# The inverse of the delta rule's triangular matrices, levelled from the left side instead of the right, on one core

## The chip, the cores and the metric

The kernel runs on one core of one Trainium2 chip. The metric is the device time of one execution of the whole program in microseconds (us). The program computes two transformer blocks one after the other; the change touches one stage of the first block, which runs twice.

## The reference, cut to what matters

The first block's mixer is a gated delta rule in chunks of 64 tokens. For each chunk, head and direction a unit lower triangular 64x64 matrix is made and a system with it is solved.

```python
def gated_delta_chunked(q, k, v, beta, g, s0):
    incl, strict = tri_masks()
    q, k, v, beta, g = map(to_chunks, (q, k, v, beta, g))
    gc = jnp.cumsum(g, axis=-1)
    decay = jnp.exp(jnp.where(incl, gc[..., :, None] - gc[..., None, :], -jnp.inf))
    kk = jnp.einsum("nbhid,nbhjd->nbhij", k, k)
    a_mat = jnp.where(strict, beta[..., :, None] * kk * decay, 0.0) + jnp.eye(CHUNK, dtype=kk.dtype)
    ...
    sol = lax.linalg.triangular_solve(a_mat, rhs, left_side=True, lower=True, unit_diagonal=True)
    ...
    def step(s, xs):
        qd, kd, u_c, w_c, qk_c, al = xs
        v_new = u_c - jnp.einsum("bhck,bhkv->bhcv", w_c, s)
        ...
```

There are 8 heads of width 128, 256 context tokens and 512 latent tokens (12 chunks), and two directions, of which the second reads the tokens backwards.

## The kernel before

**Stages.** The heads are worked in two groups of four (hg 0 and 1). For each group `pe_chunks`, `act_chunks`, ... project, convolve and normalise; then `pe_scan`, `act_scan`, `dve_scan` and `pool_scan` run the delta rule. The change lies in the scans alone. All the engines' queues are written out by hand, each engine in program order; semaphores join them.

**Units.** A scan has 12 units, s = 0 to 11. A unit is one chunk of each direction for four heads: the chunk of one direction lies on partitions 0 to 63, that of the other on 64 to 127, so that a tile of 128x256 holds eight 64x64 matrices. A block of matmuls over them is 8 instructions of 64x64 (4 heads by 2 halves), each shown by the profile as two records of fp32, 16 records a block. Units 0 to 3 are context, 4 to 11 (`lat`) are latent and have two phases more (`qk` and `pt`). Each unit uses one of four sets of tiles: XY (X in columns 0 to 255, Y = X transposed in 256 to 511), BA (A, and beside it its transpose AT), EP (E, PP), EQ and R. In the rows all of these are called `u`; the identity, masks and other constants are `con`, the level masks `lvl`.

**What a unit does.** `ga` and `kk` make A: POOL `ga`, PE k times k and a sum of gates, ACT exp (`ev`), POOL times beta (`eb`), DVE product (`a`). `tr` makes the start of the inverse: POOL X = A times the level 0 mask (`x0`), DVE X += identity (`xy` 0), and beside them PE turns A (block `at`) and ACT copies AT from PSUM to SBUF. Then five levels, each in two phases. `("ax", lv)`: PE multiplies A by X, DVE masks it into E (`ev`). `("xy", lv)`: PE makes both products of E with the inverse (two blocks, 32 records), DVE adds them to X and Y. In `("ax", 1)` PE also turns X (block `y0`), and ACT copies that to Y. After the levels `ks`, `vn` and `out` apply the inverse, and update the states SS (`ss` in the rows: 8 SCALAR_TENSOR_TENSOR on DVE for a unit).

**Order.** `gdn_order` sets one order of phases for all engines. It works in turns: in a turn each live unit does its next phase, oldest first, and the newest unit is last. Two to four units are live. So in the turn in which a new unit has its `tr`, the blocks and DVE steps of the older units stand ahead of it in every queue.

**PSUM.** The 8 banks are a ring: `K.ps.take` waits until the readers of the bank's last but eighth user have let go.

Of the kernel before, what the change touches and what calls it, by code (L numbers as in the profile page):

```python
# [373 lines left out]
class Kernel:  # L374
# [958 lines left out]
    def pe_scan(self, hg):  # L1333
        K, pe, hs = self, self.pe, range(4)
        H = lambda ap, h: ap[:, h * 128:h * 128 + 128]
        Q = lambda ap, h: ap[:, h * 64:h * 64 + 64]
        act, dve, pool, id_ = K.act, K.dve, K.pool, K.con("id")
        rows = [slice(64 * hf, 64 * hf + 64) for hf in range(2)]
        pe.wait_ge(K.ended("chunks", hg), dve.at("nbe"))
        for s, ph in gdn_order():  # L1340
            par, lat, (XY, BA, EP, EQ, R) = K.unit(s)
            z, inc, pair = (hg, s), K.con(f"inc{par}"), K.pair(s)
            X, Y, A, AT, E, PP = XY[:, 0:256], XY[:, 256:512], BA[:, 0:256], BA[:, 256:512], EP[:, 0:256], EP[:, 256:512]
            tok = [slice(c * 64, c * 64 + 64) for _, _, c in pair]
            if ph == "kk":
                b = K.ps.take(pe, "kk", *z)
# [6 lines left out]
            elif ph == "qk":  # L1353
                b = K.ps.take(pe, "gq", *z)
                for h in hs:
                    pe.mm(H(b, h), K.col(K.gg, s, hg, h).broadcast_to([128, 128]), inc)
                pe.mark("gq", *z)
                b = K.ps.take(pe, "qk", *z)
                for h in hs:
                    for d, hf, c in pair:  # L1360
                        pe.mm(Q(b, h)[rows[hf], :], K.QT[:, h, (c - 4) * 64:(c - 3) * 64], K.KT[:, h, tok[d]])
                pe.mark("qk", *z)
            elif ph == "tr":
                if s == 0:
                    K.pe_keep(3, "ramp", hg)
                b = K.ps.take(pe, "at", *z)
                pe.wait_ge(dve.at("a", *z))
                for h in hs:
                    for r in rows:
                        pe.mm(Q(b, h)[r, :], Q(A, h)[r, :], id_[r, r])  # L1370
                pe.mark("at", *z)
            elif ph == "pt":
                b = K.ps.take(pe, "pt", *z)
                pe.wait_ge(dve.at("p", *z))
                for h in hs:
                    for r in rows:
                        pe.mm(Q(b, h)[r, :], Q(PP, h)[r, :], id_[r, r])
                pe.mark("pt", *z)
            elif ph[0] == "ax":
                lv = ph[1]  # L1380
                b = K.ps.take(pe, "ax", *z, lv)
                pe.wait_ge(act.at("at", *z), dve.at("xy", *z, lv - 1))
                for h in hs:
                    for r in rows:
                        pe.mm(Q(b, h)[r, :], Q(AT, h)[r, :], Q(X, h)[r, :])
                pe.mark("ax", *z, lv)
                if lv == 1:
                    b = K.ps.take(pe, "y0", *z)
                    for h in hs:
                        for r in rows:  # L1390
                            pe.mm(Q(b, h)[r, :], Q(X, h)[r, :], id_[r, r])
                    pe.mark("y0", *z)
            elif ph[0] == "xy":
                lv = ph[1]
                b = K.ps.take(pe, "xy", *z, lv)
                pe.wait_ge(dve.at("ev", *z, lv), act.at("y0", *z))
                for h in hs if lv < 5 else ():
                    for r in rows:
                        pe.mm(Q(b, h)[r, :], Q(Y, h)[r, :], Q(E, h)[r, :])
                for h in hs:  # L1400
                    for r in rows:
                        pe.mm(Q(b, 4 + h)[r, :], Q(E, h)[r, :], Q(Y, h)[r, :])
                pe.mark("xy", *z, lv)
            elif ph == "ks":
                b = K.ps.take(pe, "ks", *z)
                pe.wait_ge(dve.at("s", hg, s - 1))
                for h in hs:
                    for d, hf, c in pair:
                        pe.mm(H(b, h)[rows[hf], :], K.KT[:, h, tok[d]], H(K.SS[:, d, :], h))
                pe.mark("ks", *z)  # L1410
            elif ph == "vn":
                b = K.ps.take(pe, "vn", *z)
                pe.wait_ge(act.at("bv", *z) if s == 0 else dve.at("r", *z), dve.at("xy", *z, 5))
                for h in hs:
                    for r in rows:
                        pe.mm(H(b, h)[r, :], Q(Y, h)[r, :], H(R, h)[r, :])
                pe.mark("vn", *z)
                if lat:
                    b = [K.ps.take(pe, "o", *z, d) for d in range(2)]
                    pe.wait_ge(pool.at("q", *z))  # L1420
                    for h in hs:
                        for d, hf, c in pair:
                            pe.mm(Q(b[d], h), H(K.SS[:, d, :], h), EQ[:, h * 128 + hf * 64:h * 128 + hf * 64 + 64], h == 0, False,
                                  skip=True)
                    pe.mark("os", *z)
            elif ph == "out":
                if s < 11:
                    b = [K.ps.take(pe, "s", *z, d) for d in range(2)]
                    pe.wait_ge(dve.at("vd", *z))
                    for h in hs:  # L1430
                        for d, hf, c in pair:
                            pe.mm(H(b[d], h), K.KM[rows[hf], c // 2, h * 128:h * 128 + 128], H(R, h)[rows[hf], :])
                    pe.mark("s", *z)
                if lat:
                    b = [K.ps["o", hg, s, d] for d in range(2)]
                    pe.wait_ge(act.at("vn", *z), act.at("pt", *z))
                    for h in hs:
                        for d, hf, c in pair:
                            pe.mm(Q(b[d], h), H(BA, h)[rows[hf], :], Q(PP, h)[rows[hf], :], False, h == 3, skip=True)
                    pe.mark("o", *z)  # L1440
                pe.mark("unit", *z)
# [7 lines left out]
    def act_scan(self, hg):  # L1449
# [3 lines left out]
        for s, ph in gdn_order():  # L1453
# [8 lines left out]
                act.a(EQ, K.ps[("gq", *z)], ACT.Exp).then_inc(act("eq", *z), 1)  # L1462
                act.also("ps", "gq", *z)
            elif ph == "tr":
                act.wait_ge(pe.at("at", *z))
                act.cp(BA[:, 256:512], K.ps[("at", *z)][:, 0:256]).then_inc(act("at", *z), 1)
                act.also("ps", "at", *z)
            elif ph == "pt":
                act.wait_ge(pe.at("pt", *z))
                act.cp(EP[:, 256:512], K.ps[("pt", *z)][:, 0:256]).then_inc(act("pt", *z), 1)  # L1470
                act.also("ps", "pt", *z)
            elif ph[0] == "ax":
                h = ph[1] - 1
                if h == 0:
                    act.wait_ge(pe.at("y0", *z))
                    act.cp(XY[:, 256:512], K.ps[("y0", *z)][:, 0:256]).then_inc(act("y0", *z), 1)
                    act.also("ps", "y0", *z)
                for d, hf, c in K.pair(s) if h < 4 else ():
                    r = slice(64 * hf, 64 * hf + 64)
                    v, o = K.VM[r, c // 2, h * 128:h * 128 + 128], R[r, h * 128:h * 128 + 128]  # L1480
# [15 lines left out]
    def dve_scan(self, hg):  # L1496
# [5 lines left out]
        for s, ph in gdn_order():  # L1502
# [15 lines left out]
            elif ph[0] == "ax":  # L1518
                lv = ph[1]
                dve.wait_ge(pe.at("ax", *z, lv), dve.at("p" if lat else "a", *z) if lv == 1 else pe.at("xy", *z, lv - 1))  # L1520
                b, m = K.ps[("ax", *z, lv)][:, 0:256], K.lvl[:, lv * 2 + par, :]
                dve.tt(q4(E), q4(b), bc4(m), ALU.mult).then_inc(dve("ev", *z, lv), 1)
                dve.also("ps", "ax", *z, lv)
            elif ph[0] == "xy":
# [1881 lines left out]
```

## Time and profile before

| | us |
|---|---|
| median of 3 runs | 3894.75 (3884.72 to 3899.01) |
| the profiled execution, its span | 3889.4 |
| scan of group 0, about 254 to 461 us of the span | 207 |
| scan of group 1, about 595 to 804 us of the span | 209 |

The profiled execution has no time of its own beside its span. The scans are 416 us of 3889, and in each 12 units are inverted. The rest (projections, attention, feed-forward) has none of the changed lines. The profile of a scan is read by its timeline, since all matmuls are recorded at one line, that of a helper (L208), as are the two-operand steps (L239) and the activations (L227).

### The profile page before, as it was taken

What the parts mean: (1) busy time and instruction counts of PE and PEld (TensorE: products, weight loads), DVE (VectorE), ACT (ScalarE), POOL (GpSimd) and SP (SyncE); (2) the same over time, 40 slices, a digit from 0 to 9 for tenths busy, and PEclk for the clock granted to TensorE, in tenths of its full rate; (3) what the DMA queues carried; (4) which work ended last, traced back from release to release, by engine and by line L of the source; (5) the groups of instructions that cost most, each with busy time, mean ns of one, the idle gap of its engine ahead of it and who ended that gap; (6) DMA issues with size and microseconds to landing.
All of it is one profiled execution on the core that took longest, in us unless ns stands there. A gap on an engine that the chain in (4) does not pass through costs nothing.

```text
span 3889.4 us, 60956 instructions
## 1 busy us (share of the span) xinstructions
PE 3713.0 (95%) x25674; PEld 3011.8 (77%) x25674; DVE 1933.2 (50%) x2996; ACT 1516.2 (39%) x2548; POOL 845.8 (22%) x842
## 2 busy tenths in 40 slices
PE   6999899999999999998999999999999899999999
PEld 4678787987888757786888788876778688878887
DVE  6656555535444565745243543447565533454343
ACT  5533233323323356735233432235575522343222
POOL 1222122121111133442110120203344321002120
PEclk8999999989999999999999999999999999999999
DMA  6310030012222202111224122221111122222222
GB/s 240 121 43 3 19 70 3 3 64 105 97 96 96 71 28 76 61 60 49 94 96 137 63 93 98 98 82 39 66 60 60 35 96 98 103 92 98 95 96 91
DMA packets 81543, 300.88 MB, mean 77 GB/s; under 512 B 8824, under 2 KB 9976, under 8 KB 80504
## 3 DMA queue, kind: packets, MB, share of 16 engines
q1 hardware_dynamic: 80240, 294.90, 21.8%
q10 hardware_dynamic: 1032, 2.10, 0.5%
q8 instruction: 203, 3.33, 0.3%
q14 instruction: 68, 0.56, 0.0%
HBM read 292.76 MB, written 4.19 MB: 76 GB/s over the span
## 4 chain that ended last, share of the span: by engine, by line
PE 74%; DVE 11%; ACT 6%; issue 5%; POOL 3%; DMA 1%; SPq 0%; DVEq 0%; POOLq 0%; ACTq 0%
PE ps L208 73%; DVE wlo L239 1%; DVE he L247 1%; ACT whi L227 1%; DVE ac L247 1%; PE ps L213 1%; ACT ha L227 1%; POOL p L243 1%; DVE hc L2476 1%; ACT L227 1%; ACT wp L228 1%; DVE ss L247 1%; DVE ws L247 1%; DVE ha L239 1%; DVE sml L1944 0%
## 5 line engine op out<-in xcount | busy, mean ns | idle before, releaser
L239 DVE TENSOR_TENSOR wlo<-wraw,whi 128x1024 fp32r<-128x1024 f32 x537 | 689.8, 1289 | 777.4 <-ACT whi L227 776.7
L208 PE MATMUL ps<-hh,whi 128*128 128x512 f32 x1840 | 732.0, 398 | 6.5 <-ACT hh L227 2.1
L208 PE MATMUL ps<-hl,whi 128*128 128x512 f32 x1840 | 722.6, 393 | 0.0
L208 PE MATMUL ps<-hh,wlo 128*128 128x512 f32 x1840 | 722.0, 392 | 0.0
L227 ACT ACTIVATE whi<-wraw 128x1024 fp32r<-128x1024 f32 x537 | 559.6, 1049 | 207.7 <-PE ps L208 171.8
L208 PEld LDWEIGHTS ps<-hh,whi 128*128 128x128 f32 x1840 | 348.9, 190 | 90.9 <-ACT hh L227 7.7
L208 PEld LDWEIGHTS ps<-hh,wlo 128*128 128x128 f32 x1840 | 349.1, 190 | 74.2
L208 PEld LDWEIGHTS ps<-hl,whi 128*128 128x128 f32 x1840 | 349.5, 190 | 70.2
L208 PE MATMUL ps<-u,u 64*64 64x64 f32 (+2 forms) x6016 | 223.7, 226 | 25.5 <-DVE u L239 15.4
L208 PEld LDWEIGHTS ps<-u,u 64*64 64x64 f32 (+1 forms) x6016 | 204.7, 137 | 41.6 <-DVE u L239 19.4
L239 POOL TENSOR_TENSOR sml<-sml,con 128x4 f32<-128x4 f32 (+3 forms) x36 | 66.4, 1847 | 640.3 <-DVE sml L244 579.1
L208 PE MATMUL ps<-gh,wlo 128*128 128x512 f32 x528 | 205.5, 389 | 0.0
L208 PE MATMUL ps<-gl,whi 128*128 128x512 f32 x528 | 205.5, 389 | 0.0
L208 PE MATMUL ps<-gh,whi 128*128 128x512 f32 x528 | 205.5, 389 | 0.0
L227 ACT ACTIVATE u<-ps 128x256 f32<-128x256 f32 (+1 forms) x128 | 57.6, 450 | 251.2 <-PE ps L208 185.3
L208 PE MATMUL ps<-fh,whi 128*128 128x512 f32 x352 | 137.6, 391 | 3.3 <-ACT fh L227 2.3
L208 PE MATMUL ps<-fh,wlo 128*128 128x512 f32 x352 | 137.0, 389 | 0.0
L208 PE MATMUL ps<-fl,whi 128*128 128x512 f32 x352 | 137.0, 389 | 0.0
L239 POOL TENSOR_TENSOR gl<-fv,gh 128x512 fp32r<-128x512 f32 x66 | 85.3, 1293 | 232.1 <-ACT gh L227 232.1
L239 DVE TENSOR_TENSOR x<-x,ps 128x512 f32<-128x512 f32 x64 | 44.0, 688 | 172.7 <-PE ps L208 172.7
L227 ACT ACTIVATE gh<-fv 128x512 fp32r<-128x512 f32 x66 | 41.7, 632 | 213.4 <-DVE fv L239 213.4
L239 POOL TENSOR_TENSOR fs<-fs,rb 128x512 f32<-128x512 f32 x44 | 56.9, 1293 | 301.9 <-ACT fg L227 301.9
(402 smaller groups left out, 7062.6 us busy)
## 6 DMA issues: line engine op xcount, KB each, us to landing
wraw<-weights SPq DMA_DIRECT2D x537, 512.0 KB, 3.2
x<-xT SPq DMA_DIRECT2D x2, 2048.0 KB, 9.5
bias_lines<-ln ACTq DMA_DIRECT2D x1, 2048.0 KB
xmf<-memT SPq DMA_DIRECT2D x2, 1024.0 KB, 4.7
out<-x SPq DMA_DIRECT2D x4, 512.0 KB, 2.6
bias<-bias_lines SPq DMA_DIRECT2D x1, 1536.0 KB, 8.3
con<-consts SPq DMA_DIRECT2D x1, 1379.0 KB, 16.5
ctxt<-ctxT SPq DMA_DIRECT2D x1, 1024.0 KB, 18.4
```

What stands on the lines that cost most here:

```text
L208: self.last, self.open = self.e.matmul(out, lhsT, rhs, start=start, stop=stop, skip_group_check=skip), True
L213: self.last, self.open = self.e.transpose(out, in_, idn[0:k, 0:k]), True
L227: return self.e.activation(out, in_, func, bias=bias, scale=scale)
L228: return self.e.activation(out, in_, func, bias=bias, scale=scale, accum_out=acc)
L239: return self.e.tensor_tensor(out, a, b, op)
L243: return self.e.tensor_scalar(out, a, s1, None, op0)
L247: return self.e.scalar_tensor_tensor(out=out, in0=a, scalar=s, in1=b, op0=op0, op1=op1)
L2476: dve.e.tensor_tensor_scan(C[:, r], rst[:, r], A[:, r], 0.0, ALU.mult, ALU.add).then_inc(dve("hb", *z), 1)
```

## The change

Before, PE turned A and later X, and the level's first product had AT as the stationary operand and X as the moving one, which gives A times X. After, A itself is the stationary operand and Y the moving one. That gives the transpose of X times A; the mask of the level is taken transposed to go with it (`lvl * 2 + 1 - par`, the table's mask of the other parity), and in `xy` E and X change their sides. AT is made no more. Y is now needed by the first `ax`, so X is turned in phase `tr`, in the place where A was.

```diff
             elif ph == "tr":
                 if s == 0:
                     K.pe_keep(3, "ramp", hg)
-                b = K.ps.take(pe, "at", *z)
-                pe.wait_ge(dve.at("a", *z))
+                b = K.ps.take(pe, "y0", *z)
+                pe.wait_ge(dve.at("xy", *z, 0))
                 for h in hs:
                     for r in rows:
-                        pe.mm(Q(b, h)[r, :], Q(A, h)[r, :], id_[r, r])
-                pe.mark("at", *z)
+                        pe.mm(Q(b, h)[r, :], Q(X, h)[r, :], id_[r, r])
+                pe.mark("y0", *z)
...
             elif ph[0] == "ax":
                 lv = ph[1]
                 b = K.ps.take(pe, "ax", *z, lv)
-                pe.wait_ge(act.at("at", *z), dve.at("xy", *z, lv - 1))
+                pe.wait_ge(act.at("y0", *z), dve.at("xy", *z, lv - 1))
                 for h in hs:
                     for r in rows:
-                        pe.mm(Q(b, h)[r, :], Q(AT, h)[r, :], Q(X, h)[r, :])
+                        pe.mm(Q(b, h)[r, :], Q(A, h)[r, :], Q(Y, h)[r, :])
                 pe.mark("ax", *z, lv)
-                if lv == 1:
-                    b = K.ps.take(pe, "y0", *z)
-                    for h in hs:
-                        for r in rows:
-                            pe.mm(Q(b, h)[r, :], Q(X, h)[r, :], id_[r, r])
-                    pe.mark("y0", *z)
             elif ph[0] == "xy":
                 lv = ph[1]
                 b = K.ps.take(pe, "xy", *z, lv)
-                pe.wait_ge(dve.at("ev", *z, lv), act.at("y0", *z))
+                pe.wait_ge(dve.at("ev", *z, lv))
                 for h in hs if lv < 5 else ():
                     for r in rows:
-                        pe.mm(Q(b, h)[r, :], Q(Y, h)[r, :], Q(E, h)[r, :])
+                        pe.mm(Q(b, h)[r, :], Q(E, h)[r, :], Q(X, h)[r, :])
                 for h in hs:
                     for r in rows:
-                        pe.mm(Q(b, 4 + h)[r, :], Q(E, h)[r, :], Q(Y, h)[r, :])
+                        pe.mm(Q(b, 4 + h)[r, :], Q(X, h)[r, :], Q(E, h)[r, :])
...
             elif ph == "tr":
-                act.wait_ge(pe.at("at", *z))
-                act.cp(BA[:, 256:512], K.ps[("at", *z)][:, 0:256]).then_inc(act("at", *z), 1)
-                act.also("ps", "at", *z)
+                act.wait_ge(pe.at("y0", *z))
+                act.cp(XY[:, 256:512], K.ps[("y0", *z)][:, 0:256]).then_inc(act("y0", *z), 1)
+                act.also("ps", "y0", *z)
...
             elif ph[0] == "ax":
                 h = ph[1] - 1
-                if h == 0:
-                    act.wait_ge(pe.at("y0", *z))
-                    act.cp(XY[:, 256:512], K.ps[("y0", *z)][:, 0:256]).then_inc(act("y0", *z), 1)
-                    act.also("ps", "y0", *z)
...
-                b, m = K.ps[("ax", *z, lv)][:, 0:256], K.lvl[:, lv * 2 + par, :]
+                b, m = K.ps[("ax", *z, lv)][:, 0:256], K.lvl[:, lv * 2 + 1 - par, :]
```

PE's queue in the turn in which unit 2 of group 0 has its `tr`, and the turn after it, before the change. Here `u_80`, `u_81` and `u_82` are XY, BA and EP of unit 0, `u_85` to `u_87` those of unit 1, `u_90` to `u_92` those of unit 2, `con_1` the identity.

```order
802 L208 MATMUL ps4<-u_82_130,u_80_128 64x64 x8
803 L208 MATMUL ps4<-u_80_128,u_82_130 64x64 x8
804 L208 MATMUL ps5<-u_87_135,u_85_133 64x64 x8
805 L208 MATMUL ps5<-u_85_133,u_87_135 64x64 x8
806 L208 MATMUL ps6<-con_1_49,u_91_139 64x64 x8
807 L208 MATMUL ps7<-u_80_128,u_81_129 64x64 x8
808 L208 MATMUL ps0<-u_85_133,u_86_134 64x64 x8
809 L208 MATMUL ps1<-u_90_138,u_91_139 64x64 x8
810 L208 MATMUL ps2<-con_1_49,u_90_138 64x64 x8
811 L208 MATMUL ps3<-u_80_128,u_82_130 64x64 x8
```

The same place in PE's queue after the change:

```order
800 L208 MATMUL ps2<-u_80_128,u_82_130 64x64 x8
801 L208 MATMUL ps2<-u_82_130,u_80_128 64x64 x8
802 L208 MATMUL ps3<-u_85_133,u_87_135 64x64 x8
803 L208 MATMUL ps3<-u_87_135,u_85_133 64x64 x8
804 L208 MATMUL ps4<-con_1_49,u_90_138 64x64 x8
805 L208 MATMUL ps5<-u_80_128,u_81_129 64x64 x8
806 L208 MATMUL ps6<-u_85_133,u_86_134 64x64 x8
807 L208 MATMUL ps7<-u_90_138,u_91_139 64x64 x8
808 L208 MATMUL ps0<-u_82_130,u_80_128 64x64 x8
```

The block that turned A (`u_91`) now turns X (`u_90`); the block that turned X behind the first `ax` (row 810 before) is gone.

DVE's queue at the same place, which the change leaves as it is but for the numbers of the banks (after the change):

```order
154 L239 TENSOR_TENSOR u_85_133<-u_85_133,ps3 128x512
155 L239 TENSOR_TENSOR u_90_138<-u_90_138,con_1_49 128x256
156 L239 TENSOR_TENSOR u_82_130<-ps5,lvl_40_88 128x256
157 L239 TENSOR_TENSOR u_87_135<-ps6,lvl_40_88 128x256
158 L239 TENSOR_TENSOR u_92_140<-ps7,lvl_40_88 128x256
```

Row 154 adds the products of PE's rows 802 and 803 to unit 1's X and Y; row 155 is `xy` 0 of unit 2, for which PE's row 804 now waits.

PE's queue where unit 6 has its `tr`, a latent unit, after the change. `u_80` and `u_85` are here units 4 and 5, and `u_99` R of unit 3, whose last product (of 8) with `km_52` gives the update of the states.

```order
913 L208 MATMUL ps7<-u_99_147,km_52_100 128x128
914 L208 MATMUL ps0<-u_80_128,u_82_130 64x64 x8
915 L208 MATMUL ps0<-u_82_130,u_80_128 64x64 x8
916 L208 MATMUL ps1<-u_85_133,u_86_134 64x64 x8
917 L208 MATMUL ps2<-con_1_49,u_90_138 64x64 x8
918 L208 MATMUL ps3<-u_80_128,u_81_129 64x64 x8
```

Row 917 turned A before and turns X now; what stands around it has kept its place.

## Rows read from the trace of the kernel before

**Rows 1.** The page: span, and busy time of PE in us (share) and instructions.

```profile
span 3889.4 us, 60956 instructions
PE 3713.0 (95%) x25674; PEld 3011.8 (77%) x25674; DVE 1933.2 (50%) x2996; ACT 1516.2 (39%) x2548; POOL 845.8 (22%) x842
```

**Rows 2.** Windows, the two scans: stretch, length, busy us (instructions) by engine, clock, DMA share.

```profile
254.00:461.00 207.00, 192.76 (x4414) 174.61 (x4412) 116.53 (x295) 70.25 (x172) 39.31 (x60) 0.99 0.01 3
...
595.00:804.00 209.00, 195.09 (x4414) 176.41 (x4414) 117.12 (x297) 68.44 (x169) 39.33 (x60) 0.98 0.01 3
```

**Rows 3.** Timeline, PE, eight blocks in a row: start, duration, engine, what [idle before].

```profile
280.81 4.34 PE L208 MATMUL ps<-u,u 64*64 64x64 f32 x128
```

**Rows 4.** Timeline, all engines, from unit 0's `at` to its first `xy`.

```profile
260.51 0.68 PE L208 MATMUL ps<-con,u 64*64 64x64 f32 x16
260.78 0.61 POOL L239 TENSOR_TENSOR u<-con,gg 128x256 f32<-128x256 f32 x1
260.86 0.82 DVE L239 TENSOR_TENSOR u<-u,con 128x256 f32<-128x256 f32 x1 [0.83 <-POOL u L239]
261.24 0.38 ACT L227 ACTIVATE u<-ps 128x256 f32<-128x256 f32 x1 [2.56 <-PE ps L208]
...
261.82 0.68 PE L208 MATMUL ps<-u,u 64*64 64x64 f32 x16 [0.63 <-DVE u L239]
...
262.54 0.42 DVE L239 TENSOR_TENSOR u<-ps,lvl 128x256 f32<-128x256 f32 x1 [0.86 <-PE ps L208]
...
263.53 1.15 PE L208 MATMUL ps<-u,u 64*64 64x64 f32 x32 [0.56 <-ACT u L227]
```

**Rows 5.** Timeline, unit 1: PE's `at`, DVE's `xy` 0, PE's next turn.

```profile
269.10 0.68 PE L208 MATMUL ps<-con,u 64*64 64x64 f32 x16 [0.64 <-DVE u L239]
...
269.80 0.82 DVE L239 TENSOR_TENSOR u<-u,con 128x256 f32<-128x256 f32 x1 [0.24 <-POOL u L239]
...
271.71 2.59 PE L208 MATMUL ps<-u,u 64*64 64x64 f32 x80
```

**Rows 6.** Timeline, units 2, 3, 4, 11: PE's next block behind `at`, DVE's `xy` 0.

```profile
278.79 1.75 PE L208 MATMUL ps<-u,u 64*64 64x64 f32 x48
...
279.16 0.56 DVE L239 TENSOR_TENSOR u<-u,con 128x256 f32<-128x256 f32 x1
...
290.60 1.75 PE L208 MATMUL ps<-u,u 64*64 64x64 f32 x48 [0.64 <-DVE u L239]
...
291.06 0.42 DVE L239 TENSOR_TENSOR u<-u,con 128x256 f32<-128x256 f32 x1
...
303.48 1.16 PE L208 MATMUL ps<-u,km 64*128 64x128 f32 x16
...
303.73 0.42 DVE L239 TENSOR_TENSOR u<-u,con 128x256 f32<-128x256 f32 x1
...
420.69 0.41 DVE L239 TENSOR_TENSOR u<-u,con 128x256 f32<-128x256 f32 x1
420.70 1.16 PE L208 MATMUL ps<-u,km 64*128 64x128 f32 x16
```

**Rows 7.** Timeline, unit 6: DVE's add ahead, PE's next block, DVE's `xy` 0.

```profile
334.85 0.68 DVE L239 TENSOR_TENSOR u<-u,ps 128x512 f32<-128x512 f32 x1
...
335.58 1.61 PE L208 MATMUL ps<-u,u 64*64 64x64 f32 x48 [0.84 <-DVE u L239]
...
335.78 0.41 DVE L239 TENSOR_TENSOR u<-u,con 128x256 f32<-128x256 f32 x1
```

**Rows 8.** Timeline, behind unit 4's `tr`: DVE's state update, PE's wait.

```profile
304.69 2.16 DVE L247 SCALAR_TENSOR_TENSOR ss<-ss,ex,ps 128x128 f32<-128x128 f32 x8 [0.54 <-PE ps L208]
...
307.23 2.08 PE L208 MATMUL ps<-u,u 64*64 64x64 f32 x64 [1.05 <-DVE u L239]
```

**Rows 9.** Timeline, scan of group 1: unit 1's and unit 2's `xy` 0.

```profile
610.50 0.82 DVE L239 TENSOR_TENSOR u<-u,con 128x256 f32<-128x256 f32 x1 [0.24 <-POOL u L239]
...
619.86 0.56 DVE L239 TENSOR_TENSOR u<-u,con 128x256 f32<-128x256 f32 x1
```

**Rows 10.** Windows, PE alone, the ends of both scans: busy us, clock.

```profile
795.00:800.00 5.00, 3.69 (x44) 0.67 0.02 3
...
450.00:455.00 5.00, 3.19 (x68) 1.00 0.00 0
```

More of the change, by code:

```diff
@@ L1342, in pe_scan @@
             z, inc, pair = (hg, s), K.con(f"inc{par}"), K.pair(s)
-            X, Y, A, AT, E, PP = XY[:, 0:256], XY[:, 256:512], BA[:, 0:256], BA[:, 256:512], EP[:, 0:256], EP[:, 256:512]
+            X, Y, A, E, PP = XY[:, 0:256], XY[:, 256:512], BA[:, 0:256], EP[:, 0:256], EP[:, 256:512]
             tok = [slice(c * 64, c * 64 + 64) for _, _, c in pair]
```

## Prediction, made before the changed kernel was run

> **What bounds the kernel now.** The page comes first. PE is busy in 95% of the span, DVE in half of it [rows 1]. Then the two scans, where alone the change lies: PE is busy 192.8 of 207 us in the first and 195.1 of 209 in the second, DVE 117 in each, ACT 70, POOL 39, and DMA does nothing [rows 2]. So in a scan PE sets the time nearly everywhere; some 14 us of each scan it waits. What a change is worth there is then read at the places where PE waits or will wait, in the timeline, and not from shares.
>
> **What is removed.** One block of 8 matmuls per unit, the second transpose. Its price is PE's pitch in a run without a gap: eight blocks take 4.34 us from the first start to the last end [rows 3], and since a block's last record ends some 0.15 us after the next one may start, that is 0.52 us a block. 24 units give 12.5 us. ACT loses one copy of 0.38 us per unit [rows 4]; ACT is busy a third of the scan, and I count that at nothing: PE hides it, and where the copy is waited for it is counted below. The banks: a unit takes one bank less, so each take looks at a user further back and never at a nearer one. That can't cost, and the half-microsecond waits of PE for banks that ACT or DVE still read stay, because the same pairs of users stand eight takes apart. Nothing.
>
> **What is exchanged at one price.** The level products have the same shapes with their operands swapped: blocks of 8 matmuls of 64x64 as before. The first `ax` waits for ACT's copy of Y instead of the copy of AT. The mask is another slice of the same table. Nothing each.
>
> **What is added: a wait.** The transpose that stays stands in phase `tr` and took A. A was ready a turn earlier. Now it takes X, and X is ready only behind POOL's mask step and DVE's `xy` 0. DVE's `xy` 0 is the last step of its turn: ahead of it in DVE's queue are the steps that read the older units' blocks of that same turn, and those blocks stand directly ahead of the transpose on PE. So PE must stop until DVE has caught up with it and has done one step more. Behind the waiting transpose on PE's queue stand the next turn's blocks of all the older units, which would be ready.
>
> How long it stops can be read from the trace of before, since up to that point nothing has changed. For unit 2, `xy` 0 runs from 279.16 to 279.72, while PE had begun the transpose at 278.33 and the block behind it at 278.79 [rows 6]. After the change the transpose begins at 279.72 plus the hand-over, which I take as 0.05: in unit 6 DVE's add ends at 335.53 and PE, which waited for it, starts at 335.58 [rows 7]. Then the transpose takes 0.52 until the next block starts, and in the next turn `y0`'s 0.52 is saved. The two cancel. What a unit costs is therefore a simple difference:
>
> (end of `xy` 0 + 0.05) minus the start of what followed `at` on PE before.
>
> Where PE already waited behind `at`, that start is the end of the old wait, so the old wait is absorbed and not counted twice (0.64 us in unit 3 and 0.84 in unit 6).
> - Unit 2: 279.77 - 278.79 = 0.98 [rows 6].
> - Unit 3: 291.53 - 290.60 = 0.93 [rows 6].
> - Unit 4: 304.20 - 303.48 = 0.72 [rows 6].
> - Unit 6: 336.24 - 335.58 = 0.66 [rows 7].
> - Unit 11: 421.15 - 420.70 = 0.45 [rows 6].
> - Units 5, 7, 8, 9, 10, from the same two kinds of row: 0.92, 0.46, 0.73, 0.82, 0.67.
>
> Units 2 to 11: 7.34 us.
>
> Units 0 and 1 start with few or no others beside them, so that the chain itself counts. Unit 0: `xy` 0 ends at 261.68, the transpose starts at 261.73. ACT's copy starts 0.73 after the block's start and takes 0.38 (260.51 to 261.24), so it ends at 262.84 and `ax` 1 starts at about 262.90, where it was 261.82. DVE's masking starts 0.72 later and takes 0.42, to 264.04; the first `xy` starts at 264.09 instead of 263.53 [rows 4]. That is 0.56, and not the full 1.1, because before the change that `xy` waited for the copy of Y. Unit 1: `xy` 0 ends at 270.62, transpose 270.67, ACT's copy to 271.78, `ax` 1 at 271.85, and the next turn at 272.37 instead of 271.71 [rows 5]: 0.66.
>
> A scan gains 7.34 + 0.56 + 0.66 = 8.6 us of length. The second scan repeats the first 340.7 us later: unit 1 at 610.50 for 269.80, unit 2 at 619.86 for 279.16 [rows 9]. Only its unit 0 has a longer wait already, and I count it at 0.3 less. Together 16.8 us: a gross stall of about 29 us and a saving of 12.5.
>
> **Does anything give it back?** Only a later wait of PE for something that ran on during the stall. The largest wait in the middle, 1.05 us before 307.23, is for DVE behind the state update, which begins only when PE has made its product behind the transpose (303.48, then DVE at 304.69) [rows 6, 8]; it moves with the stall and gives nothing. The same holds for the waits in the last turns of a scan. I count nothing, with up to 3 us per scan as the bound on that side.
>
> **A price that could be larger.** Since PE now waits for `xy` 0, its length counts. It takes 0.42 us in the middle of the scan [rows 6], but 0.82 in units 0 and 1, where POOL works beside it (260.78 to 261.39 beside 260.86 to 261.68) [rows 4, 5]. The units above are priced with their own lengths. Between the ends, all as now and all at 0.82, I take the first, because DVE and POOL keep their order up to that point; the other end adds 0.4 us for 20 units, 8 us, and belongs to the range.
> The Trainium skill states as much (Advanced Engine Details and Errata, section Miscellaneous Facts): POOL shares a port with DVE and conflicts with DVE steps that have two inputs in SBUF, as `xy` 0 has. By that rule too the sum changes only if the two meet more often.
>
> **The sum.** On the profiled execution: 3889.4 + 16.8 = 3906.2. The median of the runs is 5.3 us above that span, so 3911.5, or 0.43% slower. A measurement of this kernel can tell about 0.5% (19.5 us) from no change, so this is a loss that falls just inside "the same".
>
> **Rivals.**
> 1. *The removed block is not gained, the stall is paid in full.* In the turn behind `tr`, `y0` lay between the first `ax` and the next turn, and DVE used that time for three masking steps. If PE then waits for DVE by what `y0` took, the loss is the gross one: 16.8 + 12.5 = 29 us, 3924. For it: DVE is the second busiest engine, and the stall sends it three blocks in a row. Against it: before, DVE itself stood idle for PE in those turns, and three masks take 1.4 us against PE's 1.6 for three blocks. It decides once DVE is late by more than 0.5 us there. Chance 0.17.
> 2. *The wait is hidden.* If `xy` 0 is done when PE comes to the transpose, only the saving is left: 3894.75 - 12.5 = 3882. That needs POOL and DVE some 1.2 us earlier in every unit, and no row shows that in any unit. Partly true (half of the stalls given back) it would be about 3897. Chance 0.12 for both.
> 3. *The clock.* The new stalls are 24 gaps of 1 to 2 us. The granted clock was 0.67 in 795 to 800 us, after two gaps of PE near 1.5 us, yet 1.00 in the same kind of stretch in the other scan, with PE busy only 3.2 of 5 us [rows 10]. If a third of the stalls were followed by such a stretch, each at some 1.5 us, that is 12 us more: 3924. Chance 0.06. The Trainium skill (TensorE: Matmul & The Clock Gate, A second HAM failure mode) says that frequent short idles between groups of matmuls let the clock oscillate between its two levels; by that rule the change would be slower by this. The trace of before mostly speaks against it, since PE there idles often and the clock stays at 0.98 to 0.99 [rows 2].
> 4. *It doesn't do what it says.* The queue of the new kernel has 24 blocks fewer, so that is excluded but for the time of the swapped operands. Chance 0.02.
>
> **How the numbers follow.** My case (3905 to 3919) has 0.63. The range takes in the case of half the stalls given back at its lower end and the full stall at its upper: 3895 to 3925. Slower by over 0.5% means above 3914.2: the full stall, the clock, and the upper third of my case, which reaches there by a stall 0.1 us longer in each unit, 0.35 together. Within 0.5%: 0.62. Faster by over 0.5% would need more than the whole saving: 0.03.
>
> **What would show it.** Right: in the timeline PE has 24 blocks of identity with `u` fewer, and the remaining one of `tr` has an idle of 0.9 to 2 us before it, released by DVE; unit 2's transpose about 1.4 us later after its predecessor than now; scans of about 215.5 and 217 us; no change elsewhere; DVE, ACT and POOL shifted, not longer. Wrong: waits of PE before the second turn's blocks (rival 1); transposes without idle ahead (rival 2); clock under 0.95 within a scan (rival 3); or `xy` 0 at 0.8 us in the middle of a scan.

## The result and the profile after

| | median, us | runs |
|---|---|---|
| before | 3896.88 | 3884.72 to 3899.77, 4 runs |
| after | 3921.89 | 3916.77 to 3933.36, 4 runs |
| ratio | 1.0063, 95% interval 1.0044 to 1.0082 | |

The changed kernel is slower by 25 us (17 to 32). Six further runs of it beside other kernels gave 1.0076 (1.0060 to 1.0092). The prediction was 3911.5 with 16.8 us of loss, and a range of 3895 to 3925.

The page of the profiled execution after, in the same two lines as [rows 1]:

```profile
span 3925.0 us, 60124 instructions
PE 3722.0 (95%) x25290; PEld 3017.4 (77%) x25290; DVE 1933.5 (49%) x2996; ACT 1505.9 (38%) x2524; POOL 845.1 (22%) x842
```

PE has 384 records fewer (24 blocks of 16), ACT 24 instructions fewer, DVE and POOL have all of theirs. The windows of the two scans, each from POOL's first `ga` to the end of PE's last product on `u` (columns: stretch, length, busy us of PE, PEld, DVE, ACT, POOL, clock, DMA share, GB/s), answer to [rows 2]:

```profile
255.37:475.16 219.79, 192.64 (x4223) 173.57 (x4223) 116.90 (x295) 64.39 (x158) 39.30 (x60) 0.97 0.01 3
608.90:833.40 224.50, 198.01 (x4222) 178.14 (x4222) 116.88 (x295) 63.44 (x157) 39.26 (x60) 0.94 0.01 3
```

Cut in the same way the scans of before took 206.4 and 208.4 us, at a clock of 0.99 and 0.98. So the scans took 29.6 us of the 35.6 by which the two profiled executions differ, and the stretch between them is the same to 0.1 us (133.65 and 133.71). Another 5.6 us lie behind the second scan (3085.0 and 3090.6 us), where no line was changed; among the profiled executions of all kernels below, that stretch varies from 3080.0 to 3095.1 us, so these 5.6 say little about the change. In the scans two things grew: PE's idleness (27 us a scan instead of some 14) and the time at a lower clock.

**The stop.** PE's waits for DVE's steps on `u` in both scans, before and after (columns: who waited, for whom, us in total, times, longest):

```profile
PE ps L208 <- DVE u L239: 16.6, 19, 1.8
...
PE ps L208 <- DVE u L239: 45.1, 36, 2.2
```

28.5 us more. Where they are is seen in the timeline of unit 2's `tr`, which answers to [rows 6]:

```profile
281.10 1.27 DVE L239 TENSOR_TENSOR u<-u,ps 128x512 f32<-128x512 f32 x2
281.26 0.73 POOL L239 TENSOR_TENSOR u<-u,lvl 128x256 f32<-128x256 f32 x1 [0.54 <-DVE u L239]
281.95 0.61 POOL L239 TENSOR_TENSOR u<-con,gg 128x256 f32<-128x256 f32 x1
282.29 0.55 DVE L239 TENSOR_TENSOR u<-u,con 128x256 f32<-128x256 f32 x1
282.90 0.68 PE L208 MATMUL ps<-con,u 64*64 64x64 f32 x16 [1.27 <-DVE u L239]
283.41 1.27 PE L208 MATMUL ps<-u,u 64*64 64x64 f32 x38
```

DVE adds the products of the older units' blocks (281.10, two of them), then does `xy` 0 (282.29 to 282.84), and the transpose starts 0.06 us behind it; it had been free to start 1.27 us sooner. The next turn's blocks (283.41) stand behind it. All 24 units show this. In the first scan the stops ahead of the transpose are, for units 1 to 11: 2.20, 1.27, 2.14, 1.13, 1.98, 1.98, 0.86, 1.12, 1.13, 0.99, 0.86 us; in the second they are the same within 0.01. From unit 7's transpose to that of unit 11 the clock is at 2.4 GHz in both kernels. The two transposes before, and the two after:

```profile
349.44 0.63 PE L208 MATMUL ps<-con,u 64*64 64x64 f32 x16
...
420.14 0.63 PE L208 MATMUL ps<-con,u 64*64 64x64 f32 x16
...
360.70 0.68 PE L208 MATMUL ps<-con,u 64*64 64x64 f32 x16 [0.86 <-DVE u L239]
...
434.35 0.68 PE L208 MATMUL ps<-con,u 64*64 64x64 f32 x16 [0.86 <-DVE u L239]
```

73.65 us after, 70.70 before. The prediction's sum for the four units between (7 to 10) is 0.46 + 0.73 + 0.82 + 0.67 = 2.68; measured 2.95.

**The clock.** The other part is not in the stops. PE's timeline behind unit 5's `tr`:

```profile
329.62 0.68 PE L208 MATMUL ps<-con,u 64*64 64x64 f32 x16 [1.98 <-DVE u L239]
330.14 1.40 PE L208 MATMUL ps<-u,u 64*64 64x64 f32 x32
...
331.32 1.07 PE L208 MATMUL ps<-con,u 64*64 64x64 f32 x16
```

Two windows of 5 us, behind the stop of unit 5 and behind that of unit 3:

```profile
331.00:336.00 5.00, 5.00 (x98) 4.48 (x97) 2.32 (x7) 1.74 (x5) 0.00 (x0) 0.68 0.01 3
296.00:301.00 5.00, 5.00 (x126) 5.00 (x122) 2.02 (x5) 1.87 (x5) 0.00 (x0) 0.66 0.01 3
```

A block that takes 0.63 elsewhere takes 1.07 at 331.32, and the mean granted clock is 0.68 and 0.66 in these windows: for a part of them TensorE was at 1.2 GHz, its lower level. In windows of 5 us over the middle of both scans (units 1 to 11) such dips stand behind the stops of units 1, 3 and 5 in the first scan and of units 3, 5 and 6 in the second. Those are stops of 1.98 to 2.20 us, of which there are eight, and no dip stands behind a stop of 0.86 to 1.27. The second profiled execution of the same kernel (`again`, below) has them behind units 1, 3 and 5 and behind 3 and 5. Before, there was no dip between unit 1's `tr` and unit 11's in either scan. Each of these dips costs some 1.7 us of clock (in the window at 296, 5.00 x (1 - 0.66)), so they take some 10 us in the one execution and 8.5 in the other.

The length of a stop alone doesn't decide. In the last turns of every scan of every kernel here, the one before the change too, PE stops once for 1.80 us; of these 22 stops 14 are followed by a dip and 8 are not (before: 795.08, the dip of [rows 10], and 454.37, none).

**Two columns for what follows.** The clock varies from run to run (before: 0.975 to 0.983), and with it the time. I therefore give beside the time of each kernel its mean granted clock over all its runs, and the mean of time times granted clock, which is about what it would take at full clock. It is an approximation (a lower clock costs nothing while PE idles), but a fair one here: the scans of `no_wait` below took 204.63 and 200.64 us at lost clock (1 - clock, times length) of 6.1 and 2.0 us, so that one us of lost clock is about one us of time. The clocks have three digits, which is good to 2 us; the 52 runs of before, in three sets beside the other kernels, give 3812.1, 3813.3 and 3813.8, together 3812.9.

| kernel | runs | mean us | clock | time x clock | less before | ratio of times, 95% |
|---|---|---|---|---|---|---|
| before | 52 | 3897.7 | 0.978 | 3812.9 | | |
| after, with again | 10 | 3925.3 | 0.9753 | 3828.3 | +15.4 | 1.0063, 1.0076 |
| wait_only | 5 | 3941.5 | 0.9742 | 3839.8 | +26.9 | 1.0112 (1.0095 to 1.0129) |
| no_wait | 11 | 3891.9 | 0.9767 | 3801.3 | -11.6 | 0.9987 (0.9977 to 0.9998) |
| late | 11 | 3898.4 | 0.9773 | 3809.8 | -3.1 | 0.9998 (0.9987 to 1.0009) |
| mixed | 12 | 3889.9 | 0.9779 | 3804.0 | -8.9 | 0.9982 (0.9972 to 0.9992) |
| hoist | 5 | 3918.7 | 0.9744 | 3818.4 | +5.5 | 1.0058 (1.0045 to 1.0071) |
| fill | 6 | 3919.3 | 0.9780 | 3833.1 | +20.2 | 1.0056 (1.0042 to 1.0070) |
| fill_short | 6 | 3923.7 | 0.9777 | 3836.1 | +23.2 | 1.0069 (1.0053 to 1.0084) |
| fill_long | 7 | 3917.8 | 0.9771 | 3828.3 | +15.4 | 1.0053 (1.0035 to 1.0071) |

### The profile page after: what moved, and what is told of

Same layout as the page of the kernel before. It is cut to its first block, busy times and chain, and to the rows that moved or that the text cites. A ratio compares the mean times of both kernels' runs of the same rounds, so it can differ in the third digit from the quotient of the medians.

```text
span 3925.0 us, 60124 instructions
## 1 busy us (share of the span) xinstructions
PE 3722.0 (95%) x25290; PEld 3017.4 (77%) x25290; DVE 1933.5 (49%) x2996; ACT 1505.9 (38%) x2524; POOL 845.1 (22%) x842
## 4 chain that ended last, share of the span: by engine, by line
PE 73%; DVE 11%; ACT 6%; issue 5%; POOL 3%; DMA 1%; SPq 0%; DVEq 0%; POOLq 0%; ACTq 0%
PE ps L208 72%; DVE wlo L239 1%; DVE he L247 1%; ACT whi L227 1%; DVE ac L247 1%; PE ps L213 1%; DVE hc L2466 1%; ACT ha L227 1%; DVE ss L247 1%; POOL p L243 1%; DVE u L239 1%; ACT wp L228 1%; DVE ha L239 1%; ACT L227 1%; DVE ws L247 1%
## 5 line engine op out<-in xcount | busy, mean ns | idle before, releaser
L208 PEld LDWEIGHTS ps<-u,u 64*64 64x64 f32 (+1 forms) x6016 | 210.7, 142 | 35.6 <-DVE u L239 14.2
L227 ACT ACTIVATE u<-ps 128x256 f32<-128x256 f32 (+1 forms) x104 | 48.4, 466 | 288.3 <-PE ps L208 220.4
```

What stands on the lines that cost most here:

```text
L208: self.last, self.open = self.e.matmul(out, lhsT, rhs, start=start, stop=stop, skip_group_check=skip), True
L227: return self.e.activation(out, in_, func, bias=bias, scale=scale)
```

## Experiments

The theory that the experiments test: the loss is the stop of PE behind DVE's `xy` 0 less one block, and on top of it a lower clock behind the long stops. The rivals: that the exchanged operands or the banks cost something; that PE would wait for DVE wherever the transpose stood; that the clock has nothing to do with the stops.

### One part alone: the wait

```diff
                 b = K.ps.take(pe, "at", *z)
-                pe.wait_ge(dve.at("a", *z))
+                pe.wait_ge(dve.at("a", *z), dve.at("xy", *z, 0))
```

> The kernel before with one edit: the transpose of A in phase tr waits for DVE's xy 0 as well; y0 stays where it was and nothing is saved. Theory (the wait stops PE, and the price of the changed kernel is this stall less 12.5 us for the removed block): 29 us slower than before in stall, and some 8 us more by a lower granted clock behind the stalls, so 3926 to 3935, ratio 1.0075 to 1.010; PE's waits for DVE u rise from 16.6 us by about 29. Rival (the operands' exchange or the banks cost something, the wait little): under 10 us slower, ratio under 1.003.

Measured 3943.57 median, ratio 1.0112, above the upper end of what was expected. Time times clock rose by 26.9 us against 29.3 in the sum (16.8 and 12.5), the rest is a clock of 0.974: some 16 us, where 8 were expected. PE's waits for DVE on `u` rose from 16.6 to 45.8 us, as expected. Here too dips stand in the middle of the scans, behind five of the eight stops of units 1, 3, 5 and 6 (1.98 to 2.29 us). From unit 7 to unit 11, at full clock, the kernel takes 75.51 us (367.05 to 442.56), 4.81 more than before; the sum says 2.68 + 4 x 0.52 = 4.76. So the price of the stop was read rightly, to 0.05 us in four units. The exchange of operands and the banks have no part in this kernel, and its loss is larger than that of the change: the first rival falls.

### The other part alone: the block, without the wait

```diff
                 b = K.ps.take(pe, "y0", *z)
-                pe.wait_ge(dve.at("xy", *z, 0))
+                pe.wait_ge(dve.at("a", *z))
                 for h in hs:
                     for r in rows:
-                        pe.mm(Q(b, h)[r, :], Q(X, h)[r, :], id_[r, r])
+                        pe.mm(Q(b, h)[r, :], Q(A, h)[r, :], id_[r, r])
```

> The changed kernel, but the block in phase tr turns A as it did before, without waiting for xy 0, and its copy goes to Y. Y is then the transpose of A and not of X, so the inverse is another; the work is that of the changed kernel without the wait. Theory: the removed block alone is left, 24 x 0.52 = 12.5 us faster than before, 3884, ratio 0.9968, clock in the scans 0.98 to 0.99. Rival (the swapped operands of the level products cost PE something, or the removed block lay in a wait): no faster than before, ratio 1.000 or above.

Measured 3891.26 median, ratio 0.9987: faster, but by 5 us and not by 12.5. Time times clock fell by 11.6. The windows of its two scans:

```profile
256.17:460.80 204.63, 190.36 (x4223) 172.42 (x4223) 116.42 (x295) 64.38 (x158) 39.32 (x60) 0.97 0.01 3
592.36:793.00 200.64, 187.55 (x4222) 169.08 (x4222) 116.41 (x295) 63.44 (x157) 39.30 (x60) 0.99 0.01 3
```

The same instructions in the same order take 4 us longer in the first scan, at 0.97. In that one the clock was at 0.50 from 451 to 461 us, in the last turns, behind the stop of 1.80 us that every kernel has there. The part of the expectation on the clock (0.98 to 0.99) thus failed in one scan of two. From unit 7 to 11: 68.83 us, 1.87 less than before, or 0.47 a block where I had 0.52. The two parts add up to the change: 4.81 - 1.87 = 2.94, and the change itself has 2.95; in time times clock 26.9 - 11.6 = 15.3, and the change has 15.4. No further term is seen in the change while the clock is full. The swapped operands cost nothing that the rows show: three blocks of level products take 1.61 us in this kernel (at 333.39) as in [rows 7]. The mean clock of the 11 runs is 0.9767, below the 0.978 of before, though this kernel has none of the new stops: that drop, some 6 us, has another cause, which is not known.

### The transpose where X has long been ready

For the latent units the block goes into `pt`, one turn later, on PE and ACT; context units as in the change.

```diff
             elif ph == "tr":
...
+                if not lat:
+                    turn_x(s)
...
             elif ph == "pt":
...
                 pe.mark("pt", *z)
+                turn_x(s)
```

> The changed kernel with the transpose of X one phase later, in pt, for the 16 latent units, where X has been ready for a turn; the context units as in the changed kernel. Theory: the net cost of units 4 to 11 (5.4 us a scan) and the blocks' 8 x 0.52 come back, 9.6 us a scan, 19 us in all, and 3 to 5 us more by the clock: 3922 - 23 = 3899, ratio 1.0005, between 0.999 and 1.002. Rival (PE then waits for DVE one turn later, because DVE is what is late and not the place of the transpose): half of it at most, ratio above 1.003.

Measured 3897.94 median, ratio 0.9998 (0.9987 to 1.0009), inside the expected bounds; time times clock 3809.8, 18.5 below the changed kernel where 19 was expected. The stops ahead of the latent units' transposes are gone. PE's waits for DVE's older steps have moved and grown a little: in the first scan 0.58, 1.05, 1.31, 0.33 and 0.33 us in the turns of units 4 to 10, where before there were 1.05, 0.58, 0.84 and one of 0.67, half a microsecond more in all. The rival (DVE late wherever the transpose stands) falls. The kernel only reaches the time of before, since its 8 context units still stop, among them those of 2.20 and 2.14 us; its first scan took 215.2 us at a clock of 0.94, with dips behind units 1 and 3 and others at both ends. In that scan unit 1's stop was only 1.60 us, because PE had come to it at its lower level, and the clock fell again behind it (0.71 from 281 to 286 us); so a dip can follow a shorter stop than those of the changed kernel.

### Latent units by the new product, context units as before

```diff
-                pe.wait_ge(act.at("y0", *z), dve.at("xy", *z, lv - 1))
+                pe.wait_ge(act.at("y0" if lat else "at", *z), dve.at("xy", *z, lv - 1))
                 for h in hs:
                     for r in rows:
-                        pe.mm(Q(b, h)[r, :], Q(A, h)[r, :], Q(Y, h)[r, :])
+                        pe.mm(Q(b, h)[r, :], Q(A if lat else AT, h)[r, :], Q(Y if lat else X, h)[r, :])
                 pe.mark("ax", *z, lv)
+                if lv == 1 and not lat:
+                    turn_x(s)
```

> Context units (4 a scan) as before the change, with AT and y0 in ax 1; latent units (8 a scan) by the changed product, with the transpose of X in pt. Theory: no unit is left with a new stall, and 16 blocks of 0.52 us are saved: 8.3 us faster than before at the same clock, time times granted clock 3804 against 3812 of before and 3810 of the kernel with the transpose in pt everywhere; 3888 to 3891, ratio 0.998. Rival (the swapped product costs something by itself, or the saving only pays where PE had stalled): no faster than before, time times clock 3810 or more.

Measured 3890.22 median, ratio 0.9982 (0.9972 to 0.9992), time times clock 3804.0, where 3804 was expected: faster than both kernels. That it fits to the microsecond is more than the clocks' three digits can show. Its scans:

```profile
264.58:467.72 203.14, 188.31 (x4287) 171.03 (x4287) 116.39 (x295) 66.14 (x162) 39.33 (x60) 0.99 0.01 3
598.08:801.70 203.62, 189.97 (x4286) 171.54 (x4286) 116.43 (x295) 65.17 (x161) 39.31 (x60) 0.98 0.01 3
```

PE in the turn behind unit 6's `tr`: `pt` and the transpose of X are one run of 32 records, without a stop between or behind them.

```profile
344.84 1.61 PE L208 MATMUL ps<-u,u 64*64 64x64 f32 x48 [1.31 <-DVE u L239]
346.29 1.10 PE L208 MATMUL ps<-con,u 64*64 64x64 f32 x32
347.22 1.57 PE L208 MATMUL ps<-u,u 64*64 64x64 f32 x48
```

The stop of 1.31 us ahead of them is the wait for DVE's older steps that was there before, 0.84 us in [rows 7], and longer by 0.47: the block that `tr` no longer has on PE had been hidden in it. Here the block is not gained, and in the turn of unit 5 it isn't either (a stop of 1.05 us for one of 0.58). Unit 4 gives one back: the block in `pt` now fills 0.47 us of the 1.05 us of [rows 8]. PE's waits for DVE on `u` are 19.9 us in all, 3.3 more than before.

### DVE's `xy` 0 one place earlier

```diff
+        order = gdn_order()
+        for i in [i for i, x in enumerate(order) if x[1] == "tr" and x[0] > 0]:
+            order[i - 1], order[i] = order[i], order[i - 1]
-        for s, ph in gdn_order():
+        for s, ph in order:
```

> The changed kernel with DVE's xy 0 put one place earlier in DVE's queue alone, ahead of the last older unit's step of that turn (but for unit 0). Theory (the length of PE's stop is set by the steps that stand ahead of xy 0 on DVE): each stop of units 2 to 11 becomes shorter by the step passed, 0.25 to 1.05 us, 5.5 us a scan, 11 in all; time times clock 3816 against 3827 of the changed kernel; about 3910, ratio 1.003 to 1.004. Rival (POOL's x0 or the hand-overs set it): no change of the stops, ratio 1.006; or the steps that were passed are now late themselves and PE waits for them instead: the stops shorter, other waits longer by as much.

Measured 3919.28 median, ratio 1.0058; expected was 1.003 to 1.004. Time times clock 3818.4, against 3816 expected and 3828.3 of the change, so the stops did shrink nearly as read. Those of units 2 to 11 in the first scan are now 1.27, 1.65, 0.19, 1.74, 1.74, 0.39, 0.19, none, 0.66 and 0.39 us; the rows of units 4 and 10:

```profile
308.43 0.68 PE L208 MATMUL ps<-con,u 64*64 64x64 f32 x16 [0.19 <-DVE u L239]
...
412.36 0.68 PE L208 MATMUL ps<-con,u 64*64 64x64 f32 x16 [0.66 <-DVE u L239]
```

5.2 us less a scan where 5.5 was read from the rows of before. Only in unit 2 did nothing move. PE's waits for DVE on `u` fell from 45.1 to 36.1 us in all, so at most 1.5 of the 10.5 us came back as other waits. The steps ahead of `xy` 0 on DVE therefore set the stop. What did not come is the time: the clock was 0.9744, the lowest but one of the table, with stops of 2.20 and 1.74 us still there. In its profile the dips stand about units 0 and 1 (2.2 us) and in the last turns of both scans, and none behind the stops of 1.65 and 1.74. Part of the clock is lost outside the scans: the stretch behind the second one took 3095.1 us, 4.5 more than in the changed kernel, though no line differs there. All five runs have a clock of 0.974 or 0.975, so it isn't one bad execution; the cause stays open.

### PE kept at work during the stops

Three kernels put matmuls on the identity, whose result nobody reads, ahead of the waiting transpose. `fill` has 16 of them in all units but 0, `fill_short` 8, each in a bank of their own; `fill_long` has 24 in units 1, 3, 5 and 6 alone, in the transpose's own bank:

```diff
                 b = K.ps.take(pe, "y0", *z)
+                for _ in range(3 if s in (1, 3, 5, 6) else 0):
+                    for h in hs:
+                        for r in rows:
+                            pe.mm(Q(b, h)[r, :], id_[r, r], id_[r, r])
                 pe.wait_ge(dve.at("xy", *z, 0))
```

> The changed kernel with 16 matmuls of 64x64 on the identity ahead of every waiting transpose but unit 0's, about 1.0 us of PE work into a bank that nobody reads, where PE otherwise waits 0.9 to 2.2 us. It leaves the wait and takes away most of PE's idleness there. Theory A (behind the stalls the clock falls to its lower level and that costs some 8 us above the 16.8 of the stalls): the clock in both scans goes back to 0.98 to 0.99 without dips in the stretches behind the stalls of units 3, 5 and 6, and the time falls by 4 to 8 us against the changed kernel, ratio to before about 1.0045. Theory B (the dips come with something else): dips as before the fill, ratio 1.006 to 1.007, since the filling costs 0 to 3 us where the stall is shorter than it.

> The changed kernel with 8 matmuls of 64x64 on the identity ahead of each waiting transpose but unit 0's, 0.52 us of PE work that fits into each of the stops (0.86 us the shortest). Theory A (PE's idleness at the stops is what lowers the clock): nothing is paid for the filling, time times clock stays at 3827, and the mean granted clock of the runs rises from 0.9755 to 0.977 or more: 3915 to 3920, ratio 1.005. Theory B: the clock stays at 0.9755, time 3923.

> The changed kernel itself once more, beside the others of this call, for its clock and its spread: mean time 3921 to 3924 and mean granted clock 0.975 to 0.976 if the lower clock belongs to the kernel; 3915 and 0.978 if it was the luck of four runs. Time times clock 3827 in either case.

> The changed kernel with 24 matmuls of 64x64 on the identity (1.56 us) written to the transpose's own bank ahead of its wait, in units 1, 3, 5 and 6 alone, where PE stops for 1.98 to 2.20 us; no bank is taken for them, so that the ring's order stays (in the two kernels filled before, one more bank a unit brought PE new waits for ACT and DVE). Theory A (the clock falls behind the long stops): the stops there are 0.4 to 0.6 us, nothing is paid, time times clock 3828 as in the changed kernel, but no dip of the clock behind units 1, 3, 5, 6, mean clock of the runs 0.977 to 0.978, time 3915 to 3918, ratio 1.005. Theory B (the dips have another cause): time 3923 to 3926, clock 0.975.

| | clock of the runs | time x clock | median us |
|---|---|---|---|
| after and again | 0.9755 and 0.9752 | 3827.3 and 3829.0 | 3921.89 and 3926.80 |
| fill | 0.9780 | 3833.1 | 3918.66 |
| fill_short | 0.9777 | 3836.1 | 3925.06 |
| fill_long | 0.9771 | 3828.3 | 3917.94 |

The lower clock belongs to the changed kernel: `again` has 0.9752 as the first four runs had 0.9755, at nearly the same product (its mean time, 3926.5 us, is above the 3921 to 3924 expected). In all three filled kernels it rises, by 0.0018 to 0.0027, which is about 7 to 11 us, and in none of them does a dip stand behind the transposes of units 1, 3, 5 and 6 (24 places, where `after` and `again` have 11 dips in 16). But in the first two the filling was not free, and both missed their expected ratio (1.0056 for about 1.0045, 1.0069 for 1.005): `fill_short` was expected to leave the product at 3827 and has 8 us more. Its waits show half of it; the changed kernel has 1.9 us (4 times) for ACT's `ot` and 1.3 us (twice) for DVE's:

```profile
PE ps L208 <- DVE u L239: 37.4, 36, 2.3
PE ps L208 <- ACT ot L227: 3.9, 8, 0.5
...
PE ps L208 <- DVE ot L239: 3.5, 2, 1.7
```

The one bank more for each unit brings the ring round sooner, and PE meets banks that ACT or DVE still read: 4.2 us in all. The rest of the 8 I have not traced. In both kernels the longer wait for DVE's `ot`, 1.75 us in the last turns of each scan, is itself followed by a dip in all four scans, which is part of why the clock of `fill`'s scans stayed at 0.97 where 0.98 to 0.99 was expected. So those two don't test the clock cleanly. `fill_long` does: no bank, product 3828.3 as in the change, median 3917.94 (expected 3915 to 3918), the stops of units 1, 3, 5 and 6 at 0.80, 0.65, 0.58 and 0.58 us (expected 0.4 to 0.6). Behind unit 5:

```profile
330.18 1.57 PE L208 MATMUL ps<-con 64*64 64x64 f32 x48
...
332.33 0.68 PE L208 MATMUL ps<-con,u 64*64 64x64 f32 x16 [0.58 <-DVE u L239]
332.84 1.10 PE L208 MATMUL ps<-u,u 64*64 64x64 f32 x32
...
333.78 0.63 PE L208 MATMUL ps<-con,u 64*64 64x64 f32 x16
```

The window over the same stretch:

```profile
331.00:336.00 5.00, 4.42 (x127) 4.04 (x125) 2.64 (x8) 2.36 (x6) 0.61 (x1) 1.00 0.01 3
```

The block that took 1.07 us takes 0.63, the same stretch has a clock of 1.00, and there is no dip from unit 1 to unit 11 in either scan. That the dips in the middle of the scans come from PE's idleness in the long stops is thereby shown by the traces. The times alone would not show it: the interval of the ratio (1.0035 to 1.0071) overlaps both of the changed kernel's. Its clock of 0.9771 is still below the 0.9785 that before had beside it, and near the 0.9767 of `no_wait`: dips in the last turns of a scan are left, and what decides whether they come there is open.

## Why the prediction was right, and where not

- **What bounds the kernel.** Right: what PE's queue gained and lost in the scans accounts for the change at full clock (15.3 of 15.4 us); the stretch between the scans kept its length. "No change elsewhere" did not hold for the profiled execution, by the 5.6 us behind the second scan.
- **The removed block.** 0.52 us was a little high; `no_wait` gives 0.47 in the middle of the scan. The trace of before had that price already: unit 2's transpose starts at 278.33 and what follows it at 278.79, 0.46 us later. 24 blocks: 11.6 us at full clock for 12.5 expected.
- **The stop.** Right where the full clock lets it be checked, in units 7 to 11 (4.76 forecast, 4.81 measured). From the end of `xy` 0 in the trace of before I had 29 us gross for all units; `wait_only` lost 26.9 at full clock. The waits of PE for DVE rose by 28.5, but that they come so near is partly luck: some idleness before was absorbed, and an idle is counted from the modelled end of a block's last record, some 0.15 us after the next block could have started. The hand-over of 0.05 is 0.06 in the rows.
- **The balance.** 16.8 was the sum; 15.4 is what ten runs show in time times clock. No row shows a wait that gave the stop back, as forecast.
- **Rival 1 (the block not gained)** fell: in the turns behind `tr` no new wait came, and `wait_only` and `no_wait` add up to the change (15.3 for 15.4 us). Its time, 3924, was near the measured one by accident.
- **Rival 2 (hidden)** fell: all 24 stops are there. **Rival 4** (the change not doing what it says) too.
- **Rival 3 (the clock)** is what the prediction under-rated, with 0.06 and a price of zero in the likeliest case. Some 10 us of the 25 are the clock, and it is the term by which the measured loss exceeds 0.5%. The price that it gave to this rival, 12 us for eight dips of 1.5, was near: there were six dips, and five in the other execution, of 1.7 us each, 10 and 8.5 us. What `fill_long` gives back is 7.5 us of mean time. So most of the clock's part is shown to come from the long stops, and the rest of it is open. The working has the step that failed in it: "the old wait is absorbed and not counted twice". That holds for time. But where an old wait of 0.64 or 0.58 or 0.84 us behind the transpose and a new one ahead of it became a single one, the stop became 2 us long (units 3, 5 and 6), and it is behind those, and behind unit 1's of 2.20 us, that the clock falls. I looked at the sum of the idle time and at [rows 10], which come from stretches in which PE was busy 64 and 74% of the time, and not at the length of one stop.
- **The Trainium skill** (TensorE: Matmul & The Clock Gate, A second HAM failure mode) says that short idles between groups of matmuls make the clock oscillate. The traces agree in part: in the two executions of the changed kernel dips came behind 11 of 16 stops of 1.98 to 2.20 us, and behind none of 0.86 to 1.27. The forecast's rule on the shared port (the Trainium skill, Advanced Engine Details and Errata, Miscellaneous Facts) found nothing more to do: `xy` 0 kept its 0.41 to 0.42 us in units 3 to 11 and its 0.82 in units 0 and 1.
- **The chances.** I gave 0.62 to a change within 0.5% and 0.35 to slower; it is slower by 0.63% (0.44 to 0.82). So the case that had most of the chance did not come. The range held the first median (3921.9) by 3 us, which is in part luck, while the later one (3926.8) lies just above it.

## What to carry to other kernels

When an edit saves an instruction on the busy engine but moves the wait of its fellow to a later producer, take the trace of before and subtract, at each place, the time at which the engine now goes on from the end of that producer; look where the producer stands in its own engine's queue, since it may come last of a turn that itself follows the busy engine. Here the block was worth 0.5 us and the wait 1.2, and the remedy was to move the block to where its input had been ready for a turn, and to leave those units as they were for which there is no such place. When waits merge, their sum can stay the same and the engine's clock still fall: look at the longest stop, not only at the sum.

## What the runs showed of the hardware that was not expected

- In the middle of the scans, behind 11 of 16 single stops of PE of 1.98 to 2.20 us, its granted clock fell for some microseconds (0.66 to 0.72 in a window of 5 us that holds the whole dip), and a block of 64x64 products went from 0.63 to 1.07 us. With 1.56 us of idle products put into that stop it stayed at 1.00. Behind stops of 1.65 and 1.74 us (six, in `hoist`) it stayed too, while in the last turns, where the stop is 1.80 us, it fell in 14 of 22 cases.
- The clock differs between executions of one kernel (before: 0.975 to 0.983 in 52 runs), and the time goes with it (3907 to 3884 us). Time times granted clock has a spread of 1.0 to 3.2 us (one standard deviation) within a kernel here, and told kernels apart whose times are alike: `hoist` and `fill_long` have mean times of 3918.7 and 3917.8 us, and products of 3818.4 and 3828.3.
- One more PSUM bank for each unit, in a ring of eight, brought about 2 us a scan of new waits for banks still being read (two more of 0.48 us for ACT, and one that grew from 0.67 to 1.75 for DVE), though the added work itself fitted into a stop.
